# A hybrid encoder with a mixture-of-experts stage: five places for split weight pieces instead of three

## The reference, cut to what matters

```python
def swiglu(h, w1, w3, w2):
    return (jax.nn.silu(h @ w1) * (h @ w3)) @ w2

def moe_swiglu(h, w_router, w1, w3, w2):
    logits = (h @ w_router).astype(jnp.float32)
    top_v, top_i = lax.top_k(logits, TOP_K)
    wts = jax.nn.softmax(top_v, axis=-1)
    combine = jnp.sum(jax.nn.one_hot(top_i, N_EXPERTS) * wts[..., None], axis=-2)
    out = jnp.zeros_like(h)
    for e in range(N_EXPERTS):
        out = out + combine[..., e:e + 1] * swiglu(h, w1[e], w3[e], w2[e])
    return out
```

## Time and profile before

| | us |
|---|---|
| median of 3 runs | 1623.9 (1622.59 to 1624.29) |
| the profiled execution | 1622.44 |
| its span, first to last instruction | 1620.6 |
| PE busy in the span | 1576.3 (97%) |
| DVE busy | 1278.0 (79%) |
| ACT busy | 1057.4 (65%) |
| the 328 splits of the expert stage on DVE (L2381) | 738.9, 2.286 each |
| the 328 copies of it on ACT (L1726) | 624.0, 1.917 each |

### The profile page before, as it was taken

How to read it: one execution, slowest core, us unless ns; L and a number is a source line. 1 busy time by engine, 2 the same in 40 slices (tenths; PEclk the granted TensorE clock), 3 DMA queues, 4 the chain that set the end, 5 groups by cost and what they waited for, 6 DMA issues and landing times.

```text
span 1620.6 us, 21022 instructions
## 1 busy us (share of the span) xinstructions
PE 1576.3 (97%) x8224; PEld 1335.5 (82%) x8224; DVE 1278.0 (79%) x1204; ACT 1057.4 (65%) x988; POOL 28.6 (2%) x69
## 2 busy tenths in 40 slices
PE   9999999999999999999999999989999999999997
PEld 8988888999989888787877788777788777788885
DVE  7575666555576756689899988899888999888997
ACT  6555445333355554567788877788777888777774
POOL 1000000000000000001000000000000000000100
PEclk9999999999999999999999999999999999999998
DMA  7754478977455535669999999999999999999992
GB/s 239 223 185 142 143 250 279 303 245 233 127 165 174 181 117 182 250 259 364 423 421 420 421 419 391 368 422 420 422 398 374 401 420 421 412 394 352 409 397 114
DMA packets 143112, 497.48 MB, mean 307 GB/s; under 512 B 8534, under 2 KB 64400, under 8 KB 100000
## 3 DMA queue, kind: packets, MB, share of 16 engines
q1 hardware_dynamic: 137008, 479.23, 78.1%
q0 software_dynamic: 2624, 8.45, 1.5%
q10 hardware_dynamic: 3376, 8.39, 1.4%
HBM read 476.64 MB, written 19.40 MB: 306 GB/s over the span
## 4 chain that ended last, share of the span: by engine, by line
PE 71%; DVE 20%; ACT 4%; issue 4%; DMA 1%; ACTq 0%; POOL 0%; DVEq 0%; POOLq 0%
PE bank L730 21%; DVE wlo L2381 14%; PE bank L1187 14%; PE bank L1230 13%; PE bank L901 9%; PE bank L1191 7%; ACT whi L1726 2%; ACT whi L1493 1%; PE bank L720 1%; DVE wlo L1915 1%; PE bank L1015 1%; PE bank L1210 1%; PE bank L1206 1%; DMA hn<-in_mem 1%; ACT pbuf L1628 0%
## 5 line engine op out<-in xcount | busy, mean ns | idle before, releaser
L2381 DVE TENSOR_TENSOR wlo<-raw,whi 128x2048 fp32r<-128x2048 f32 x328 | 738.9, 2286 | 67.4 <-ACT whi L1726 67.1
L1726 ACT ACTIVATE whi<-raw 128x2048 fp32r<-128x2048 f32 x328 | 624.0, 1917 | 161.5 <-PE bank L1191 83.8
L1915 DVE TENSOR_TENSOR wlo<-raw,whi 128x2048 fp32r<-128x2048 f32 (+3 forms) x121 | 259.3, 2148 | 178.6 <-ACT whi L1493 177.2
L1187 PE MATMUL bank<-whi,yT_hi 128*128 128x512 f32 x896 | 311.9, 396 | 0.0
L1493 ACT ACTIVATE whi<-raw 128x2048 fp32r<-128x2048 f32 (+3 forms) x121 | 217.8, 1801 | 137.7 <-PE bank L730 101.3
L1191 PE MATMUL bank<-wlo,yT_hi 128*128 128x512 f32 x896 | 240.5, 390 | 0.1
L1187 PE MATMUL bank<-whi,yT_lo 128*128 128x512 f32 x560 | 216.5, 390 | 0.0
L1230 PE MATMUL bank<-whi,yT_hi 128*128 128x512 f32 x448 | 180.4, 403 | 26.1 <-DVE yT_hi L2412 16.0
L1191 PEld LDWEIGHTS bank<-wlo,yT_hi 128*128 128x128 f32 x896 | 167.8, 188 | 36.9 <-DVE wlo L2381 1.4
L1187 PEld LDWEIGHTS bank<-whi,yT_hi 128*128 128x128 f32 x896 | 166.7, 188 | 33.1
L1230 PE MATMUL bank<-wlo,yT_hi 128*128 128x512 f32 x448 | 175.9, 393 | 0.0
(11 more groups left out here) (323 smaller groups left out, 2059.2 us busy)
## 6 DMA issues: line engine op xcount, KB each, us to landing
raw<-in_moe_w SPq DMA_DIRECT2D x336, 1024.0 KB, 8.5
raw<-in_w_in SPq DMA_DIRECT2D x36, 1024.0 KB, 5.2
raw<-in_dense_w SPq DMA_DIRECT2D x30, 1024.0 KB, 6.6
raw<-in_w_br SPq DMA_DIRECT2D x12, 1024.0 KB, 5.0
rows_by_slot<-qxT SPq DMA_DIRECT2D x23, 512.0 KB, 7.2
raw<-in_w_out SPq DMA_DIRECT2D x8, 1024.0 KB, 5.0
raw<-in_w_mkv SPq DMA_DIRECT2D x6, 1024.0 KB, 8.4
cqkv<-rows_by_slot ACTq DMA_DIRECT2D x7, 512.0 KB, 7.9
```

What stands on the lines that cost most here:

```text
L1187: nc.tensor.matmul(b[:, :], hselT[a][:, half, tok(k)], w[:, k, :], start=(half + k + a == 0), stop=False)
L1726: nc.scalar.activation(whi[:, (E0 + n) % SPLIT, :], raw[:, n % RAW, :], ACT.Copy).then_inc(hi_ready, 1)
L1915: V.tensor_tensor(wlo[:, m % SPLIT, 0:size], raw[:, pieces[n][1], 0:size], whi[:, m % SPLIT, 0:size].bitcast(F32), ALU.subtract).then_inc( ...
L2381: V.tensor_tensor(wlo[:, s, :], raw[:, n % RAW, :], whi[:, s, :].bitcast(F32), ALU.subtract).then_inc(lo_ready, 1)
```

## The change

`whi` and `wlo` stay as they are, and two more places are taken from tiles that the expert stage doesn't use otherwise: `mT` is place 3, `hT` place 4. A plan (`e_home`) gives every piece its place, the one that has been held longest, and `e_before` the piece that lay there; ACT's copy of piece n now waits for that one, n-5 for most pieces, n-4 from piece 290 on (`HT_END`: `hT` is used again in the last expert) and n-3 in the overflow loop that runs only if an expert has more tokens than fit. The first pieces that use `mT` and `hT` are 8 and 9.

`e_room` has a new argument. With `near` it counts, as before, pieces up to three behind PE's mark; without it, it counts by the new places. `near` is true in a light expert, in blocks up to 3 and in the last block of a heavy expert ahead of a light one (`is_near`). Nothing is added to or taken from the work: all instructions of PE are the same and in the same order, and SP's too; on ACT and DVE the same instructions change places. DVE gets one wait more in the last expert (for the last piece in `hT`).

```diff
--- before.py
+++ after.py
@@ -585,6 +585,22 @@
             piece(("e", DEPTH - 1, n), RAW, e_source(*e_items[n][1:], 0))
         e_base = [16 * sum(len(p[2]) for p in pieces if p[1] == s and p[0][0] != "e") for s in range(RAW)]
 
+        spare_parts = [[v[:, :, :].rearrange("p k s -> p (k s)") for v in pair] for pair in (mT, hT)]
+        FIRST_SPARE, HT_END = HEAD + EARLY, N_E - PER_E - HEAD
+        e_home, e_before, holds = [], [], {}
+        for n in range(N_E + PER_E):
+            if n < FIRST_SPARE:
+                home = (E0 + n) % SPLIT
+            elif n >= N_E:
+                home = n % SPLIT
+            else:
+                homes = [h for h in range(SPLIT + 2) if h <= SPLIT or n < HT_END]
+                home = min(homes, key=lambda h: holds.get(h, h - 2 * SPLIT))
+            e_home.append(home)
+            e_before.append(n - SPLIT if n >= N_E else holds.get(home))
+            holds[home] = n
+        last_in_hT = max(n for n in range(N_E) if e_home[n] == SPLIT + 1)
+
         def raw_wait(eng, n):
 
             s = pieces[n][1]
@@ -674,14 +690,25 @@
                     return m
             return len(split_order)
 
-        def e_room(phase, kind, n):
+        def held_part(n, part):
+
+            home = e_home[n]
+            return (whi, wlo)[part][:, home, :] if home < SPLIT else spare_parts[home - SPLIT][part]
+
+        def e_room(phase, kind, n, near=False):
 
             limit = marks[phase, kind, n][0]
             start, end = (N_E, N_E + PER_E) if phase == "over" else (0, N_E)
             i = start + SPLIT
-            while i < end and marks["item", i - SPLIT][0] < limit:
+            while i < end and marks.get(("item", i - SPLIT if near else e_before[i]), (0, 0))[0] < limit:
                 i += 1
             return i
+
+        def is_near(phase, b):
+
+            if phase == "over":
+                return False
+            return light[phase] or b <= 3 or (b >= NM - 1 and phase < LAST and light[phase + 1])
 
         def light_block(p, b):
             return sum(light[:p]) * NM + b + 1
@@ -1157,11 +1184,11 @@
                 extra = [("piece", "e", DEPTH - 1, n)] if n < HEAD + EARLY else []
                 mark(ins, ("item", n), *extra, *[(phase,) + i for i in names])
 
-            def e_part(tile, ready, n, j):
+            def e_part(part, ready, n, j):
 
                 pe.wait_ge(ready, E0 + n + 1 + PER_E * j)
                 k = 2 if e_items[n][1] == "w2" else 4
-                return tile[:, (E0 + n) % SPLIT, :].rearrange("p (k c) -> p k c", k=k)
+                return held_part(n, part).rearrange("p (k c) -> p k c", k=k)
 
             def is_light(phase):
                 return phase != "over" and light[phase]
...
@@ -1720,10 +1747,13 @@
                 for n in range(n_done, end):
                     act.wait_ge(raw_in[n % RAW], e_base[n % RAW] + 16 * (n // RAW + 1) + 16 * (PER_E // RAW) * j)
                     if N_E <= n < N_E + SPLIT:
+
                         reached(act, "over", j)
+                    elif e_before[n] is None:
+                        reached(act, ("out", DEPTH - 1, T - 1, 1))
                     else:
-                        reached(act, ("item", n - SPLIT), j)
-                    nc.scalar.activation(whi[:, (E0 + n) % SPLIT, :], raw[:, n % RAW, :], ACT.Copy).then_inc(hi_ready, 1)
+                        reached(act, ("item", e_before[n]), j)
+                    nc.scalar.activation(held_part(n, 0), raw[:, n % RAW, :], ACT.Copy).then_inc(hi_ready, 1)
                 n_done = max(n_done, end)
 
             def is_light(phase):
@@ -1778,9 +1808,9 @@
             def blocks(phase, j=0):
 
                 for b_ in range(1, NM):
-                    e_hi(e_room(phase, "e1", b_), j)
+                    e_hi(e_room(phase, "e1", b_, is_near(phase, b_)), j)
                     if is_light(phase):
-                        e_hi(e_room(phase, "eT", b_ - 1), j)
+                        e_hi(e_room(phase, "eT", b_ - 1, True))
                         silu_folded(phase, b_ - 1)
                     e_silu(phase, b_, j)
                     if b_ == 1 and phase != "over" and phase and light[phase - 1]:
@@ -1791,9 +1821,9 @@
                         if phase:
                             reached(act, (phase, "rows", 1))
                         act.dma_start(row_in_slot, rows_by_slot[phase + 1]).then_inc(slots_moved, 16)
-                    e_hi(e_room(phase, "eT", b_ - 1), j)
+                    e_hi(e_room(phase, "eT", b_ - 1, is_near(phase, b_)), j)
                     if is_light(phase):
-                        e_hi(e_room(phase, "e3", b_))
+                        e_hi(e_room(phase, "e3", b_, True))
                         copy_gate(phase, b_)
                     else:
                         hidden_hi(phase, b_ - 1, j)
@@ -1823,16 +1853,16 @@
             for p in range(NE - 1):
                 blocks(p)
 
-                e_hi(e_room(p, "e3", NM - 1))
+                e_hi(e_room(p, "e3", NM - 1, is_near(p, NM - 1)))
                 reached(act, (p, "e3", NM - 1))
                 rows_hi_part(p + 1)
-                e_hi(e_room(p + 1, "e1", 0))
+                e_hi(e_room(p + 1, "e1", 0, True))
                 if light[p]:
-                    e_hi(e_room(p, "eT", NM - 1))
+                    e_hi(e_room(p, "eT", NM - 1, True))
                     silu_folded(p, NM - 1)
                 e_silu(p + 1, 0)
                 if not light[p]:
-                    e_hi(e_room(p, "eT", NM - 1))
+                    e_hi(e_room(p, "eT", NM - 1, light[p + 1]))
                     hidden_hi(p, NM - 1)
                 if light[p + 1]:
                     e_hi(e_room(p + 1, "e3", 0))
@@ -2376,9 +2406,8 @@
 
                 nonlocal n_done
                 for n in range(n_done, end):
-                    s = (E0 + n) % SPLIT
                     dve.wait_ge(hi_ready, E0 + n + 1 + PER_E * j)
-                    V.tensor_tensor(wlo[:, s, :], raw[:, n % RAW, :], whi[:, s, :].bitcast(F32),
+                    V.tensor_tensor(held_part(n, 1), raw[:, n % RAW, :], held_part(n, 0).bitcast(F32),
                                     ALU.subtract).then_inc(lo_ready, 1)
                 n_done = max(n_done, end)
 
@@ -2397,7 +2426,7 @@
 
                 end = N_E + PER_E if phase == "over" else N_E
                 last = phase in (LAST, "over") and b_ == NM - 1
-                e_lo(min(e_room(phase, "eT", b_), end - 1 if last else end), j)
+                e_lo(min(e_room(phase, "eT", b_, is_near(phase, b_)), end - 1 if last else end), j)
                 b = full(dve, (phase, "eT", b_), j)
                 count = NM * (NE if phase == "over" else phase) + b_ + 1 + NM * j
                 if is_light(phase):
...
@@ -2452,14 +2482,14 @@
             def blocks(phase, j=0):
 
                 for b_ in range(1, NM):
-                    e_lo(e_room(phase, "e1", b_), j)
+                    e_lo(e_room(phase, "e1", b_, is_near(phase, b_)), j)
                     if phase == 0 and b_ == 2:
                         cap_experts()
                         order_experts()
                     if phase == 0 and b_ == 3:
                         give_slots()
                     hidden_lo(phase, b_ - 1, j)
-                    e_lo(e_room(phase, "e3", b_), j)
+                    e_lo(e_room(phase, "e3", b_, is_near(phase, b_)), j)
                     if phase == 0 and b_ in (2, 3):
                         scale_rows(b_ - 2)
                     if phase == 0 and b_ == 1:
@@ -2503,9 +2533,9 @@
             lo_parts(len(split_order))
             for p in range(NE - 1):
                 blocks(p)
-                e_lo(e_room(p + 1, "e1", 0))
+                e_lo(e_room(p + 1, "e1", 0, True))
                 hidden_lo(p, NM - 1)
-                e_lo(e_room(p + 1, "e3", 0))
+                e_lo(e_room(p + 1, "e3", 0, True))
                 hidden(p + 1, 0)
             dve.wait_ge(flag_ready, 1)
             overflow = dve.value_load(more[0:1, 0:1], min_val=0, max_val=1)
```

More of the change, by code:

```diff
@@ L1174, in up @@
                     n = nth_item[phase, kind, b_, half]
-                    w = e_part(whi, hi_ready, n, j)
+                    w = e_part(0, hi_ready, n, j)
                     if is_light(phase):
@@ L1188, in up @@
                                          start=(half + k + a == 0), stop=False)
[L1189 removed]
+                    w = e_part(1, lo_ready, n, j)
                     for k in range(4):
```

4 lines of the change are left out of this document (2 added, 2 removed).

## The result

The changed kernel takes 1642.19 us (1641.03 to 1644.42, 4 runs), the kernel before beside it 1623.36 (4 runs): a ratio of 1.0117, 95% interval 1.0105 to 1.0130. The forecast was 1636, the range 1629 to 1643. The profiled execution after is the slowest of its four, 1644.42 us with a span of 1642.7, and stands against the 1622.44 of the profiled one before: 22.0 us more in the two traces, 18.8 in the medians. One run of the last kernel of the experiments, at 2231.5 us with a mean granted clock of 0.65, is left out of its median.

A forecast was written before the change was run, and what follows sets the result against it. Light experts were taken as bound by DVE, heavy ones by PE. Three changes of experts at 5.4 us, 16.2, less 1.5, less 1.1, gave +13.6 on 1622.44, or 1636.0 us; range 1629 to 1643.

The forecast's parts named there:

- The wait: Block 5 of experts 0, 2, 4: PE's first w2 matmul waits 5.64 us for DVE's low part of the gated product.
- What stays of it: After each heavy-to-light change of experts, 3.7 us of PE's 5.64 us wait stay to the end.
- The clock: One 3.41-us stretch at half clock behind each restart, 1.7 us late: 5.4 us per change instead of 3.7.
- The one-in-six count of the short waits: Light experts: one of six PE waits of 1.6 or 1.9 us had a slow stretch; sum near three times 3.7.
- The gains: Earlier copies in expert 7 save 0.85 us, similar small steps in expert 0 save 0.65: together 1.5, bounds 0 and 2.5.
- rival D: Worse: ACT waits some 3 us for data in expert 0, two slow stretches per restart; about 1645 us, chance 0.07.
- the transfers: Behind a stall, SP sees only later frees of `raw`, with transfers that then have more time; no cost counted.
- A: DVE's lead survives into light experts: up to 13.2 us saved, priced at 8 us, 1614 us; chance 0.05.
- B: The three stalls occur but the clock holds: 3 x 3.7 = 11.1, less 2.6, gives 1631 us; chance 0.15.
- C: PE's 1.04 us of slack per light block, seven per expert, absorbs the stall: 1622 us; chance 0.05.

The follow-up runs named there:

- the last kernel of the experiments: Changed kernel with five places for both queues in the last block of experts 0, 2, 4 and three at the end of expert 6: 1618.10 us.
- the order alone: Kernel before, three places, but DVE splits two more pieces ahead of block 5's low part in experts 0, 2, 4: 1647.54 us.
- the clock held: Changed kernel with 20 identity matmuls on PE in each of the three waits: 1636.69 us.
- For expert 7 this was tested: Changed kernel, DVE at three places ahead of block 5's low part (experts 0, 2, 4), both queues at three at expert 6's end: 1618.92 us.
- the places alone: Changed kernel's five places, with ACT's and DVE's queues ordered exactly as in the kernel before: 1620.26 us.
- the kernel with the one argument mended: Changed kernel, but DVE counts three places, as ACT does, ahead of block 5's low part in experts 0, 2, 4: 1621.63 us.
- both queues in step: Changed kernel with both queues counting five places in the last block of experts 0, 2, 4, DVE's last low part included: 1618.70 us.

## Why the prediction was right, and where it was off

**The wait: right, in place, cause and size.** Predicted 5.64 us at the first w2 matmul of block 5 of experts 0, 2 and 4, released by the low part, none in expert 6; measured 5.47 in each. Every link was tested: the order alone makes it, one argument takes it away, and moving ACT's copies ahead of the rows shortens it to 3.1 us.

**What stays of it: right.** 3.7 us per change were counted behind the wait. In the trace with the clock held, PE's first use of pieces 34, 96, 180 and 258 comes 1.4, 5.7, 9.0 and 11.5 us later than before: 4.3, 3.4 and 2.5 us per change, the last 4.0 with the 1.5 us that the kernel before loses in its own slow stretch there.

**The clock: right side, size too small.** One stretch of 3.41 us and 1.7 us per restart were expected; there were two, and of them 3.7 to 6.1 us lay behind the restart. The half clock gives 3.1 + 2.2 + 1.9 = 7.2 us, the medians with and without the clock held 5.5, against 5.1 in the sum. The rule of the Trainium skill, page "TensorE: Matmul & The Clock Gate", section "HAM oscillation — how this bites in real kernels", that a PE which waits between its bursts starts each at the low clock, agrees with all nine waits of 5.5 to 5.8 us in the traces. For shorter ones the traces decide, and there the clock often stays up (last section). The one-in-six count of the short waits, by which the sum would have stayed near three times 3.7, would have been wrong.

**The gains: wrong in sign.** This is the step of the prediction that failed. I took 1.5 us off, for expert 7 (0.85) and expert 0 (0.65), with bounds of 0 and 2.5; both lose instead, 1.3 and 1.7 in the traces, a mistake of 4.5 us. Between the two profiled executions, which the sum is about, the kernel lost 22.0 us instead of 13.6: of the 8.4 us between, 4.5 are this, 3.6 the three changes of experts (18.7 instead of 16.2 - 1.1 = 15.1, mostly the clock), and 0.4 were there when the stage began. I read DVE's idle 2.54 us as a wait for a place. It wasn't: ACT's copy there stood behind its two `mv` copies and a DMA issue, in the kernel before:

```profile
1497.53 0.57 ACT L1845 ACTIVATE mv<-bank 128x512 f32<-128x512 f32 x1
1498.37 0.60 ACT L1845 ACTIVATE mv<-bank 128x512 f32<-128x512 f32 x1 [0.26 <-PE bank L1230]
1499.05 0.33 ACTq L1776 DMA_DIRECT2D y_by_slot<-mv  x1
1500.55 3.72 ACT L1726 ACTIVATE whi<-raw 128x2048 fp32r<-128x2048 f32 x2 [1.58 <-issue]
```

And I didn't ask what the farther lookahead puts in front of the next small step. Where the rule goes from three places to five, one piece more stands ahead of the low part (in expert 0 DVE splits six pieces there instead of five, 22 to 27; at the end of expert 6 four, 294 to 297, with PE waiting). For expert 7 this was tested (2.3 to 2.7 us back). For expert 0 it is argued from the queue and the 1.16-us wait, which all versions with the switch from three places to five at block 4 have and those without a switch (the places alone, the order alone) don't; moving the switch wasn't tried.

**The range: hit, with some luck.** The median of 1642.19 lies 0.8 us under the upper end of 1643, and is in it only through what was added there for the median and for rival D; the profiled execution, 1644.42, is not. That the kernel gets slower, where and by what, was forecast by its mechanism. That the time still fell inside the range, with the clock too small in the sum and the gains of the wrong sign, was luck.

**Left out: the transfers.** The prediction gave them "more time" behind a stall and stopped there. While DVE stands, `raw` isn't freed and less is loaded (249 GB/s in the slow stretch at 1041.67, 423 in a heavy block). Later ACT waits for data in a light expert:

```profile
1123.53 1.92 ACT L1756 ACTIVATE whi<-raw 128x2048 fp32r<-128x2048 f32 x1 [1.03 <-DMA raw<-in_moe_w]
1126.02 1.92 ACT L1756 ACTIVATE whi<-raw 128x2048 fp32r<-128x2048 f32 x1 [0.57 <-DMA raw<-in_moe_w]
```

Against the kernel before, the changed kernel takes on 0.6, 0.5 and 0.3 us late in the three light experts. It is tempting to put that down to the stall, but the kernel with the one argument mended has no stall and waits there too:

```profile
1108.72 1.92 ACT L1756 ACTIVATE whi<-raw 128x2048 fp32r<-128x2048 f32 x1 [1.45 <-DMA raw<-in_moe_w]
1111.22 1.92 ACT L1756 ACTIVATE whi<-raw 128x2048 fp32r<-128x2048 f32 x1 [0.57 <-DMA raw<-in_moe_w]
```

It takes on 1.0, 0.9 and 0.1 us at the same pieces. In both kernels the copies come 2.5 us apart there, which is 14.9 us for six, the pace of the loads that the prediction worked out; the kernel before has only two such waits in the light experts. What the new order saves at the start of a light expert (some 1.5 us each in experts 1 and 3, in both kernels) is in part handed back to the transfers later. No run isolates it.

**The rivals.** A (the head start works) was right that something is to be had, and wrong on its worth: with both queues in step the kernel is 4.4 us below before and 1.2 to 1.6 below the places alone, not 8 (a price that no sum in the prediction gives). The trace shows two limits, the silu that stops ACT once more and the waits for transfers; which one takes how much isn't shown. B is what the kernel with the clock held shows, at 1636.7 with the other losses. C is excluded: of 5.47 us of waiting 3.4 to 4.3 stay. D's second slow stretch came true. Its loss in expert 0 came smaller, 1.7 us instead of 3, and by another way: ACT did wait for data there (1.47 us at 770.54), but the low part that PE waited for stood behind six splits that DVE did without a gap.

## What to carry to other kernels

When two in-order queues feed each other and each is filled by a lookahead rule, the rule must give both the same bound at the same point of the work, not in the same block number. Look for a piece that the consumer has ahead of a step and the producer has behind a barrier that waits for the same engine; its price is the wait for that barrier on top of its split, here 2.3 and 2.2 us. More lookahead also puts more work in front of every small step that another engine waits for.

## What the runs showed of the hardware

- Behind waits of PE of 5.47 to 5.81 us the granted clock was 0.50 for 3.4 us once and 6.8 us eight times, nine of nine waits in three kernels. Behind waits of 3.1 us it fell in four of six (three times for 3.4 us, once for 6.8), in two kernels.
- Waits of 1.9 us were followed by 3.41 us at half clock in one of three cases in the kernel before, in none of three with the places alone, and in three of three where a stall and its slow stretch had come some 30 us earlier. A wait of 1.98 us with no stall before it was followed by one too. The wait's length alone doesn't tell.
- Matmuls that only fill a wait kept the clock at 1.00, with 1.01 us of the wait left open.
- In the light experts the loads ran at 420 GB/s with a DMA share of 1.01, and where ACT waited for them its copies came 2.5 us apart.
